# Large SBUF tiles at multiples of 512 bytes, small tables behind them, in a two-block hybrid model kernel

## The reference

```python
def swiglu(x, w_gate, w_up, w_down):
    return (jax.nn.silu(x @ w_gate) * (x @ w_up)) @ w_down
```

## Time and profile before

| | |
|---|---|
| median of 3 runs | 3486.01 us (3483.91 to 3487.39) |
| span of the profiled execution, first to last instruction | 3480.7 us |
| its own time | the profile gives the span alone; the runs' median is 5.3 us above it, their lowest 3.2 us |
| PE busy | 3359.6 us, 97%, 14384 matmuls |
| VectorE, ScalarE, GpSimd busy | 1595.7, 1170.0, 411.5 us |
| DMA | 286.04 MB, mean 82 GB/s |

### The profile page before, as it was taken

The page is one execution under the profiler, slowest core; times in us unless marked ns, Lnnn a source line. Parts: engine busy times, 40 slices in busy tenths (PEclk is TensorE's granted clock), DMA queues, the critical chain, the costliest instruction groups (busy, mean ns, idle before and its releaser), DMA issues.

```text
span 3480.7 us, 39701 instructions
## 1 busy us (share of the span) xinstructions
PE 3359.6 (97%) x14384; PEld 2578.8 (74%) x14384; DVE 1595.7 (46%) x2295; ACT 1170.0 (34%) x1726; POOL 411.5 (12%) x285
## 2 busy tenths in 40 slices
PE   7999999999999999999899999999999999899998
PEld 5888775778887788876677888565678886668886
DVE  3332489643323433288834331944343327643322
ACT  4332345432323332245533321214333214543322
POOL 1110002111100110000211100400111003111100
PEclk9999999999999999999999999999999999999999
DMA  4333231033333333332023333440223332223332
GB/s 138 93 94 97 85 79 50 3 89 96 91 96 91 90 96 92 95 79 75 1 64 88 96 92 95 99 76 31 65 86 96 93 94 85 61 79 90 96 94 76
DMA packets 420124, 286.04 MB, mean 82 GB/s; under 512 B 57416, under 2 KB 395180, under 8 KB 419884
## 3 DMA queue, kind: packets, MB, share of 16 engines
q1 hardware_dynamic: 419200, 283.62, 28.5%
q10 hardware_dynamic: 828, 1.13, 0.1%
HBM read 280.24 MB, written 4.47 MB: 82 GB/s over the span
## 4 chain that ended last, share of the span: by engine, by line
PE 90%; DVE 6%; ACT 2%; issue 2%; POOL 0%; DMA 0%; DVEq 0%; ACTq 0%; SPq 0%; POOLq 0%
PE bank L856 26%; PE bank L857 26%; PE bank L858 25%; PE bank L851 1%; PE bank L1147 1%; PE bank L1146 1%; PE bank L1165 1%; PE bank L1261 1%; PE bank L1267 1%; PE bank L1384 1%; DVE small L2257 1%; PE bank L996 0%; PE bank L998 0%; PE bank L997 0%; PE bank L1348 0%
## 5 line engine op out<-in xcount | busy, mean ns | idle before, releaser
L858 PE MATMUL bank<-xn_lo,w_hi 128*128 128x512 f32 x2800 | 1097.5, 392 | 0.0
L856 PE MATMUL bank<-xn_hi,w_hi 128*128 128x512 f32 x2496 | 1000.2, 401 | 42.8 <-DVE xn_lo L1973 20.1
L1984 DVE TENSOR_TENSOR w_lo<-wring,w_hi 128x1024 fp32r<-128x1024 f32 x478 | 594.5, 1245 | 926.0 <-ACT w_hi L1511 925.1
L857 PE MATMUL bank<-xn_hi,w_lo 128*128 128x512 f32 x2496 | 989.3, 396 | 0.0
L1511 ACT ACTIVATE w_hi<-wring 128x1024 fp32r<-128x1024 f32 x490 | 517.6, 1059 | 1194.7 <-DMA wring<-in_ffn_down 358.5
L858 PEld LDWEIGHTS bank<-xn_lo,w_hi 128*128 128x128 f32 x2800 | 528.7, 189 | 132.5
L856 PEld LDWEIGHTS bank<-xn_hi,w_hi 128*128 128x128 f32 x2496 | 470.0, 188 | 165.0 <-issue 49.4
L857 PEld LDWEIGHTS bank<-xn_hi,w_lo 128*128 128x128 f32 x2496 | 470.8, 189 | 104.6 <-issue 2.6
L857 PE MATMUL bank<-h_hi,w_lo 128*128 (+1 forms) x1056 | 420.4, 398 | 0.0
L856 PE MATMUL bank<-h_hi,w_hi 128*128 (+1 forms) x1056 | 415.8, 394 | 0.0
L858 PE MATMUL bank<-h_lo,w_hi 128*128 (+1 forms) x1056 | 415.2, 393 | 0.0
(11 more groups left out here) (382 smaller groups left out, 2913.7 us busy)
## 6 DMA issues: line engine op xcount, KB each, us to landing
wring<-in_ffn_gate SPq DMA_DIRECT2D x88, 512.0 KB, 3.8
wring<-in_ffn_up SPq DMA_DIRECT2D x88, 512.0 KB, 3.8
wring<-in_ffn_down SPq DMA_DIRECT2D x88, 512.0 KB, 3.5
wring<-in_ffn_w_gate SPq DMA_DIRECT2D x44, 512.0 KB, 3.8
wring<-in_ffn_w_up SPq DMA_DIRECT2D x44, 512.0 KB, 3.8
wring<-in_ffn_w_down SPq DMA_DIRECT2D x44, 512.0 KB, 3.5
wring<-in_w_in SPq DMA_DIRECT2D x34, 512.0 KB, 3.7
wring<-in_w_out SPq DMA_DIRECT2D x16, 512.0 KB, 3.6
```

Of the source, the lines that this page charges most:

```text
L856: nc.tensor.matmul(ps, w_hi[:, slot, t, 0:M], hi, start=start, stop=False)
L857: nc.tensor.matmul(ps, w_lo[:, slot, t, 0:M], hi, start=False, stop=False)
L858: return nc.tensor.matmul(ps, w_hi[:, slot, t, 0:M], lo, start=False, stop=stop)
L1984: nc.vector.tensor_tensor(w_lo[:, slot, :, :].rearrange("p k c -> p (k c)"), wunit[:, slot, :], w_hi[:, slot, :, :].rearrange("p k c -> p ...
```

## The change

`sb_aligned` puts a filler tensor ahead of a tile so that the tile starts at a multiple of 512 bytes. x, xn, wring, scratch, bias, arena and att_diag are allocated in this way and in this order. xn_more and hpad follow att_diag, and the constants and small tables come after them. xn_hi and `s5_wv` now lie over att_diag, and run through xn_more into hpad. All sizes, all instructions and all semaphores are as before.

```diff
--- before.py
+++ after.py
@@ -331,13 +331,26 @@
             return Sem(ctx.enter_context(nc.semaphore(name)), per, start)
 
 
-        x = sb("x", [P, KD, SEQ])
-        xn = sb("xn", [P, KD, SEQ])
+        ALIGN = 512
+
+        def sb_aligned(name, shape):
+            gap = -(-(-nc.sbuf_base // 32) * 32) % ALIGN
+            if gap:
+                ctx.enter_context(nc.sbuf_tensor(f"gap_before_{name}", [P, gap // 4], F32))
+            return sb(name, shape)
+
+        x = sb_aligned("x", [P, KD, SEQ])
+        xn = sb_aligned("xn", [P, KD, SEQ])
         y = xn
-        wring = sb("wring", [P, 2, KD, 256])
-        scratch = sb("scratch", [P, 11, SEQ])
+        wring = sb_aligned("wring", [P, 2, KD, 256])
+        scratch = sb_aligned("scratch", [P, 11, SEQ])
+        bias = sb_aligned("bias", [P, A_HEADS, SEQ])
+        arena = sb_aligned("arena", [P, 46, SEQ])
+        att_diag = sb_aligned("att_diag", [P, TB, B_HEADS, P])
+        xn_more = sb("xn_more", [P, 2, SEQ])
+        hpad = sb("hpad", [P, 2, TAPS - 1 + SEQ])
+        b_mn, b_la = xn_more[:, 0, :], xn_more[:, 1, :]
         cst = sb("cst", [P, CONST_W - PRO_W])
-        bias = sb("bias", [P, A_HEADS, SEQ])
         rows = sb("rows", [P, 4, P])
         col1 = sb("col1", [P, NR1])
         col2 = sb("col2", [P, NR2])
@@ -345,12 +358,7 @@
         cur = sb("cur", [P, NRL])
         cur_dw = sb("cur_dw", [P, TAPS * 2])
         relb = sb("relb", [64, A_HEADS])
-        hpad = sb("hpad", [P, 2, TAPS - 1 + SEQ])
-        att_diag = sb("att_diag", [P, TB, B_HEADS, P])
-        xn_more = sb("xn_more", [P, 2, SEQ])
-        b_mn, b_la = xn_more[:, 0, :], xn_more[:, 1, :]
         small = sb("small", [P, 64])
-        arena = sb("arena", [P, 46, SEQ])
         w_uq = arena[:, 29:31, 0:384]
         w_ukv = arena[:, 45, :]
         Z_HI = 36
@@ -361,7 +369,7 @@
         w_lo = over("w_lo", [P, SLOTS, KD, P], "wring")
         w_hi = over("w_hi", [P, SLOTS, KD, P], "scratch")
         xn_lo = over("xn_lo", [P, KD, SEQ], "xn")
-        xn_hi = over("xn_hi", [P, KD, SEQ], "hpad")
+        xn_hi = over("xn_hi", [P, KD, SEQ], "att_diag")
         z_hi = over("z_hi", [P, KD, SEQ], "arena", Z_HI * SEQ * 4)
         h_hi = over("h_hi", [P, NF, SEQ], "arena")
         h_lo = over("h_lo", [P, NF, SEQ], "arena", NF * SEQ * 4)
@@ -444,7 +452,7 @@
         s5_qm = scratch[:, 0:8, :].rearrange("p a (g m) -> p (a g) m", m=P)
         s5_qt = arena[:, 10:12, :].rearrange("p a (g s c) -> p (a g) s c", s=S5_L, c=SSM_C)
         s5_tm = arena[:, 22:30, :].rearrange("p a (g m) -> p (a g) m", m=P)
-        s5_wv = nc.alloc_sbuf_tensor_at("s5_wv", [P, SSM_G, P], F32, offset=at["hpad"])
+        s5_wv = nc.alloc_sbuf_tensor_at("s5_wv", [P, SSM_G, P], F32, offset=at["att_diag"])
         s5_u = [T(38), T(39), T(41), T(42)]
         s5_sin, s5_cos = bias[:, :, :], arena[:, 34:38, :]
         s5_vs, s5_yt = [T(18), T(19)], [T(43), T(44)]
```

## The result

The changed kernel takes 3417.8 us against 3486.2 (medians of 5 runs each), a ratio over all runs of 0.9814, 95% interval 0.9803 to 0.9824 (the medians alone give 0.9804): faster by 1.9 to 2.0%, 68.5 us by the medians. The forecast was 3458 us with 3447 to 3487 as its range. The direction was right, the gain was 2.4 times the 28 us forecast, and the time fell outside the range, near what rival 2 had worked out (3419).

A forecast was written before the change was run, and what follows sets the result against it. The prediction took TensorE's matmul pace as the bound. Cheaper moving-operand addresses summed to 29.2 us, taken as 28 after stage starts, other terms 0: 3486 - 28 = 3458 us, range 3447 to 3487.

The forecast's parts named there:

- rival 2: Coarser grain too: moving from 128 to 0 saves a further 8 columns on each of 11,760 matmuls, 39 us, 3419; chance 0.09.
- What bounds the kernel: TensorE busy 97% of the span, 90% of the chain; in FFNs no slack, time is matmul count times start-to-start distance.
- the 1.4 us that I took off for the starts of stages: First triples of some 13 stages wait for the activation split, so 16 triples × 6.67 ns each are lost there.
- What a remainder costs: Three-product matmuls: 690.0 ns a triple plus 3.33 ns per moving operand at 224 instead of 128, a 64-byte grain.
- The weights' remainder costs nothing: Token units are the fastest stretch though two of three weight tiles lie at 224, so weight addresses cost 0.
- The unknown, 128 to 0: Moving tiles from remainder 128 to 0, unseen in the trace: taken as 0, at most another 165 us on 11,760 matmuls.
- the sum: 2,800 triples with two moving operands at 224 save 18.7 us, 1,056 with three save 10.6 us; together 29.2 us.
- token units under 0.690: Sign of the coarser-grain rival: token-unit triples, too, fall below 0.690 us, to about 0.680.
- Rival 3: Slower: with every remainder 0, moving operand and next weight tile may meet in one bank, 39 us more, 3497; chance 0.06.
- Rival 1: No alignment effect: the 3.33 ns belongs to the tile's place, not its remainder; 3476 to 3486, likeliest 3485; chance 0.15.
- What costs nothing: Two-pass fp32 matmuls (0 to 0.2 us), ScalarE and VectorE (±3 us at most), weight loads and the start: taken as 0.

The follow-up runs named there:

- e1: Changed kernel with the weight tiles (wring, scratch) and x back at 128 bytes past a multiple of 512, other large tiles at 0; 3485.6 us.
- e5: Changed kernel with all large tiles at 128 bytes past a multiple of 512 instead of 0; 3418.5 us.
- e6: Changed kernel with all large tiles at 224 bytes past a multiple of 512 instead of 0; 3415.6 us (one run).
- e11: Kernel before the change, own tile order kept, with one filler of 160 bytes ahead of hpad, which also shifts arena; 3417.8 us.
- e8: Changed kernel with x and xn at 128, wring, scratch, bias, arena and att_diag at 224 bytes past a multiple of 512; 3466.2 us.
- e9: Changed kernel with x at 128, xn and att_diag at 192, arena at 160 bytes past a multiple of 512, weights at 0; 3496.5 us (one run).
- e3: Changed kernel with x at 128, xn and att_diag at 256, arena at 64 bytes past a multiple of 512, weights at 0; 3429.9 us (one run).

## Why the prediction was wrong, point by point

**What bounds the kernel: right.** The FFNs have no slack in PE, the gain is the pace of `split_product` alone, and counts times saved nanoseconds give 68.4 us where 61 to 69 were measured. Whether the 1.4 us that I took off for the starts of stages are real is below what the runs can tell.

**What a remainder costs: the step that failed.** The prediction had four paces and four numbers of moving operands at 224, one line went through them (690.0 + 3.33 ns each), and I read it as a cost of the moving operand's start with a 64-byte grain, with 128 as good as 0 and the weights' remainder free. All of that is false: e1 has the old time with nothing but the weights moved, and e5 and e6 have the whole gain with nothing aligned. What counts is the distance between moving operand and weights modulo 256. In that line the unknown weight remainder was nearly fixed: 128 in three stretches of four. The paces were those of distances: up had 96, 96, 0 (0.6967), down 96 three times (0.7000), the token units 160, 160, 0 (0.6900). The base of 690 was itself a slow pace. Four points that a line fits are no proof when two explanations have the same value in most of them, and the exact multiple of 8 columns made it look like one.

**"The weights' remainder costs nothing": false.** e1 moves the weights alone and pays 17 ns a triple. I had argued from the token units, the fastest stretch with weights at 224, but there the moving operand had changed too.

**The unknown, 128 to 0: mis-sized at 0.** It came out at 10 ns a triple in every stretch, 11,760 × 3.33 ns = 39 us. With the 29 us of the sum that is 68 us. The row that spoke for it was in hand, L1261 at 0.216 us for 512 column steps, 14 ns under the token units, and I put it down as unexplained. It was not the sign of a coarser grain either: e5 has every tile at 128 and the full gain. Those 39 us are part of the price of distances, which I had counted as free.

**Rival 2 had the time, not the reason.** Its sign, token units under 0.690, came true, but its mechanism, a coarser alignment, falls with e5 and e6. That the 3.33 ns a matmul which it borrowed for its second step equal the 10 ns a triple which came on top is luck. **Rival 3** (same start in every line makes operands meet) is the opposite of what holds: the same start is the free case. My argument against it, that L858 has distance 0 and lasts least, was the right clue, used only to dismiss a rival. **Rival 1** (the place of a tile): e11 leaves the tiles within 160 bytes of their places and has the gain, so place counts for nothing.

**What costs nothing: right.** The plain fp32 matmuls keep their pace, in the chain of waits of the changed kernel.

```profile
2137.22 3.45 PE bank L859 x8
...
2213.89 6.87 PE bank L1275 x16
...
2264.96 6.91 PE bank L1269 x32
```

3.45 us for 8, 6.87 for 16 and 6.91 for 32 of half the columns, as in the earlier trace rows. That each makes two passes, as the prediction has it, is inferred from the time, 0.429 us for 512 columns against 0.227 for one matmul of a triple; the trace doesn't show passes. ScalarE and VectorE, groups with busy time and mean ns:

```profile
L1992 DVE TENSOR_TENSOR w_lo<-wring,w_hi 128x1024 fp32r<-128x1024 f32 x478 | 595.5, 1247 | 887.6 <-ACT w_hi L1519 886.6
...
L1519 ACT ACTIVATE w_hi<-wring 128x1024 fp32r<-128x1024 f32 x490 | 518.0, 1059 | 1146.2 <-DMA wring<-in_ffn_down 346.7 <-DMA wring<-in_ffn_w_down 172.9 <-DMA wring<-in_ffn_up 160.2
...
L1532 ACT ACTIVATE h_hi<-arena x132 | 83.6, 633 | 207.0 <-DVE arena L2009 207.0
...
L1485 ACT ACTIVATE z_hi<-xn 128x512 fp32r<-128x512 f32 x16 | 10.1, 631 | 8.3 <-DVE xn L1971 8.2
```

633 and 631 ns, 1059 and 1247 ns, as in the earlier trace rows to 2 ns. The queue of weights kept up with the faster PE: there is no idle time before L865 or L866, and weights land in 3.6 to 3.7 us.

**The Trainium skill, TensorE: Matmul & The Clock Gate** (Step-by-step: what each phase is for) says that PE has two independent read ports, so that loading the next weights takes nothing from the matmul that runs. The runs don't show the ports, but the times don't bear out that the two reads are independent in these matmuls: the pace hangs on where the weights lie against the moving operand, from 226.7 to 234.2 ns. The 215.8 ns that the Trainium skill gives for 512 columns on the same page (Back-to-back issue gap, for an isolated matmul) is not reached by the three-product matmuls in any layout.

**What stays open.** Why 256 bytes are the period, why 64 costs a third of 32, why costs don't add up, why one layout has two paces, and where the last 12 ns go, by which 226.7 ns exceeds half the time of a plain fp32 matmul of the same width (0.429/2 us). That moving reads and weight reads meet in one part of the SBUF is a guess. No run shows the SBUF itself, and the guess alone doesn't explain the first two intervals of e8.

## What to carry to other kernels

Where three-product matmuls like these (rounded fp32, 512 columns) follow each other without a gap and each has new weights, lay moving operand and weight tiles a multiple of 256 bytes apart in the partition; alignment as such is not needed, and an odd-sized table in between cost 2.4 to 2.9% of the pace here. Other types and widths were not tried. Read the pace from starts in the timeline and compare stretches that differ in tiles alone. Before trusting a fit through them, write down for every stretch the address of both operands and ask which other function of the two has the same values.

## What the runs showed of the hardware that was not expected

- A three-product fp32r matmul of 512 columns with new weights takes 226.7 ns from start to start when moving operand and weights are 0 modulo 256 bytes apart, and 228.9 to 234.2 ns on average when a whole triple has one other distance, whatever the alignment: 160 bytes of filler are worth 68 us here.
- The cost is not a sum over matmuls. One of three at a distance of 160 costs 16.7 ns a triple (e8), two of three 10.0 ns (before, token units), all three 22.7 (e9). Two of three at 64 and one at 0 cost 20 ns (e3, input projection), three of three at 64 only 6.7 (e3, down).
- One layout can have two paces: with weights at 128 and all else at 0, the first FFN went at 0.697 and a later one at 0.700 us a triple (e1); e8 has 0.697 and 0.693.
- The plain fp32 matmuls show none of this: 6.91 us for 32 of them, 0.216 us for 256 columns each, with xn and wring 0 (e3), 64 (e9) and 128 bytes (e1) apart alike.
